# Stacking the recurrence gates of a hybrid attention and RG-LRU step on one Trainium2 core

## The reference

```python
z = rmsnorm(x, norm_mix_g) @ w_in             # 1024 -> c_q 768, c_kv 256, k_r 32, x_r 512, g_r 512
q = rmsnorm(c_q, q_norm_g) @ w_uq;  ckv = rmsnorm(c_kv, kv_norm_g);  kpe = rope(k_r)
xc = conv_b + causal_conv4(x_r)               # width 4, each channel by itself
r = sigmoid(blockdiag(xc, w_gate_a) + b_a)    # 8 diagonal blocks of 64 x 64
i = sigmoid(blockdiag(xc, w_gate_x) + b_x)
log_a = -8 * r * softplus(-lambda);  a = exp(log_a)
h_t = a_t * h_{t-1} + sqrt(1 - a_t^2) * i_t * xc_t
y = h * gelu(g_r)
```

## Time and profile before

| | |
|---|---|
| median of 3 runs | 2471.58 us (2470.5 to 2473.3) |
| the profiled execution's own time | 2471.83 us |
| its span, first to last instruction | 2470.0 us |
| TensorE busy | 2453.4 us, 99% |
| VectorE busy | 1802.2 us, 73% |
| ScalarE busy | 1218.8 us, 49% |
| GpSimd busy | 515.6 us, 21% |
| mean granted TensorE clock | 0.998 |

### The profile page before, as it was taken

One profiled execution on the slowest core, in us unless ns is written; L12 is line 12 of the kernel. 1 busy time (PEld: TensorE's weight loads), 2 busy tenths in 40 slices (PEclk: granted clock), 3 DMA queues, 4 the chain that ended last, 5 costly groups with the idle time before them and its releaser, 6 DMA issues.

```text
span 2470.0 us, 43918 instructions
## 1 busy us (share of the span) xinstructions
PE 2453.4 (99%) x17416; PEld 2369.0 (96%) x17416; DVE 1802.2 (73%) x2782; ACT 1218.8 (49%) x2197; POOL 515.6 (21%) x478
## 2 busy tenths in 40 slices
PE   9999999999999999999999999999999999999997
PEld 9999977899999999999999999779999999999997
DVE  8678767579776777677676797674887766776676
ACT  5455355535554454455524643554355544554455
POOL 0024255200112211220201232541001112211222
PEclk9999999999999999999999999999999999999999
DMA  4122201223347634663721222013135456545655
GB/s 162 53 60 73 61 11 38 82 61 109 88 92 140 122 86 99 134 120 89 226 90 53 68 64 61 11 38 95 55 115 109 88 117 131 112 88 113 131 115 171
DMA packets 104809, 230.39 MB, mean 93 GB/s; under 512 B 14832, under 2 KB 18256, under 8 KB 104608
## 3 DMA queue, kind: packets, MB, share of 16 engines
q0 software_dynamic: 43648, 89.14, 20.5%
q1 hardware_dynamic: 60816, 138.42, 17.7%
q10 hardware_dynamic: 144, 0.04, 0.0%
HBM read 144.03 MB, written 81.18 MB: 91 GB/s over the span
## 4 chain that ended last, share of the span: by engine, by line
PE 95%; DVE 2%; issue 1%; DMA 1%; ACT 0%; POOL 0%; SPq 0%; DVEq 0%; POOLq 0%
PE ps L968 28%; PE ps L1386 23%; PE ps L1337 23%; PE ps L1201 5%; PE ps L1216 5%; PE ps L1478 3%; PE ps L1271 2%; PE ps L1148 2%; PE ps L1449 1%; PE ps L1173 1%; PE ps L1080 1%; DVE xall L2828 0%; PE ps L997 0%; DVE msq L2196 0%; DVE mxp L2569 0%
## 5 line engine op out<-in xcount | busy, mean ns | idle before, releaser
L2859 DVE TENSOR_TENSOR wlo<-raw_all,whi 128x512 fp32r<-128x512 f32 (+1 forms) x420 | 270.5, 652 | 176.3 <-ACT whi L2007 173.8
L2007 ACT ACTIVATE whi<-raw_all 128x512 fp32r<-128x512 f32 (+1 forms) x420 | 248.6, 599 | 279.4 <-DVE raw_all L2992 88.0
L3359 POOL DMA_DIRECT2D x_scratch<-stage x224 | 199.7, 941 | 837.9 <-DVE stage L3002 693.4
L2060 ACT ACTIVATE stage<-ps 128x536 f32<-128x536 f32 (+1 forms) x224 | 135.4, 612 | 147.0 <-PE ps L1386 142.6
L3002 DVE TENSOR_TENSOR stage<-stage,ps 128x536 f32<-128x536 f32 (+1 forms) x168 | 118.9, 708 | 84.4 <-PE ps L1386 83.4
L1530 ACT ACTIVATE whi<-raw_all 128x1024 fp32r<-128x1024 f32 (+3 forms) x72 | 66.6, 926 | 230.4 <-PE ps L968 229.3
L2569 DVE TENSOR_REDUCE mxp<-ps 64x1 f32<-64x64 f32 (+11 forms) x384 | 140.4, 372 | 54.6 <-PE ps L1148 48.1
L968 PE MATMUL ps<-xgh,whi 128*128 128x358 f32 (+1 forms) x720 | 157.3, 327 | 0.0
L968 PE MATMUL ps<-xgl,whi 128*128 128x358 f32 (+1 forms) x720 | 156.6, 326 | 0.0
L968 PE MATMUL ps<-xgh,wlo 128*128 128x358 f32 (+1 forms) x720 | 156.6, 325 | 0.0
L968 PEld LDWEIGHTS ps<-xgl,whi 128*128 128x128 f32 x720 | 124.1, 189 | 0.0
(11 more groups left out here) (837 smaller groups left out, 7679.5 us busy)
## 6 DMA issues: line engine op xcount, KB each, us to landing
raw_all<-in_wst SPq DMA_DIRECT2D x233, 256.0 KB, 3.4
raw_all<-in_wst SPq DMA_DIRECT2D x78, 512.0 KB, 3.6
x_scratch<-stage POOLq DMA_DIRECT2D x112, 268.0 KB, 6.0
x_scratch<-stage POOLq DMA_DIRECT2D x112, 264.0 KB, 6.0
x_scratch<-xall POOLq DMA_DIRECT2D x24, 537.0 KB, 3.5
xall<-x_scratch SPq DMA_DIRECT2D x24, 537.0 KB, 9.2
xall<-in_xT SPq DMA_DIRECT2D x16, 537.0 KB, 6.8
raw_all<-in_wst POOLq DMA_DIRECT2D x30, 256.0 KB, 5.1
```

The lines of the kernel that those rows point to most:

```text
L2007: nc.scalar.activation(dst, src, ACT.Copy).then_inc(S["u_hi"], 1)
L2060: nc.scalar.activation(quarters(stage_of(L, g, i, n)[:, 0:N2]), src, ACT.Copy, scale=-1.0 if row else 1.0).then_inc(S["x_copy"], 1)
L2859: V.tensor_tensor(dst, src, hi.bitcast(F32), ALU.subtract).then_inc(S["u_lo"], 1)
L3359: pool.dma_start(x_scr[2 * i + row, :, a:b], stage_of(L, g, i, n)[:, 0:b - a], accum_op=ALU.add).then_inc(S[done], 16)
```

## The change

There are three parts.

Gates. Rows of the moving operand are stacked: `x_even` holds the high part of the even head in rows 0 to 63 and its low part in rows 64 to 127; `x_odd` holds the odd head the other way round. The weights of a head, its r and i matrices side by side, stand twice, one above the other. One pass then gives high weights by (high + low) input for both gates of one head, and a second pass gives the low weights. `gates(c)` is 2 x 2 passes. It now is one unit: the even head's result goes to banks 6 and 7 and the free end of the slot's third bank, the odd head's to the slot. The operations that split the input and read the gates work on 64 rows each, so there are more of them.

Order. Units and weight blocks now have the same numbers. `gate_r` and `gate_i` only read PSUM; the rest is `decay` and `normal`, later on ScalarE. On VectorE `split(15)`, the weights of the fourth gates, and the read of the rotary key stand ahead of `lru(2)`; the read of CQ0 stands behind it and behind `split(16)`. The rotation of the rotary key and the copies into `ckv` stand after `split(22)`; they stood before the first `cq_low`.

Roots. SUM_Y and SUM_Q use `log_rstd`, and VectorE's two reciprocals of 1074 columns per layer are gone.

The core of the diff, in which the numbers of units, the host's rearranged weights and the order on the other blocks are cut:

```diff
-U_XR, U_GR, U_GATE, U_CKV = [0, 1, 2, 3], [4, 5, 8, 9], [6, 10, 14, 18], [12, 13]
-U_KR, U_CQ = 16, [17, 20, 21, 22, 23, 24]
+U_XR, U_GR, U_GATE, U_CKV = [0, 1, 2, 3], [4, 5, 7, 8], [6, 9, 12, 15], [10, 11]
+U_KR, U_CQ = 13, [14, 16, 17, 18, 19, 20]
...
-    READ[U_GATE[_c]] = ("gate_r", _c + 1)
-    READ[U_GATE[_c] + 1] = ("gate_i", _c + 1)
+    READ[U_GATE[_c]] = ("gate_i", _c + 1)
...
                 def gates(c):
+                    u, b = U_GATE[c], B_GATE[c]
                     w("xc_lo", c + 1)
-                    for k in range(2):
-                        product(to_slot(U_GATE[c] + k), U_GATE[c] + k, B_GATE[c], 128 * k, [tok(xch)], [tok(xcl)])
+                    w("w_lo", b + 2)
+                    take(u)
+                    if c:
+                        w("gate_i", c)
+                    else:
+                        w("root", SUM_MIX)
+                    for i, part in enumerate((whi, wlo)):
+                        for dst, c0, c1 in even_gates(c, TOK):
+                            nc.tensor.matmul(dst, part[b % 2][:, 0:P], x_even[:, c0:c1], start=(i == 0), stop=(i == 1))
+                    for i, part in enumerate((whi, wlo)):
+                        for q in range(3):
+                            mm = nc.tensor.matmul(to_slot(u)(q), part[b % 2][:, P:2 * P], tok(x_odd)(q), start=(i == 0), stop=(i == 1))
+                    mm.then_inc(S["mm"], 1)
...
+                def gate(c, dst, e, bias):
+                    rest = even_gates(c, T)[1][0]
+                    nc.scalar.activation(dst[0:64, 0:SUM_END].rearrange("p (c n) -> p c n", c=2), ps[half(e), 6:8, :], ACT.Tanh, scale=0.5,
+                                         bias=bias[half(e), c:c + 1])
+                    nc.scalar.activation(dst[0:64, SUM_END:T], rest[half(e)], ACT.Tanh, scale=0.5, bias=bias[half(e), c:c + 1])
+                    return nc.scalar.activation(chunks(dst[64:128, :]), slot(U_GATE[c])[half(1 - e)], ACT.Tanh, scale=0.5, bias=bias[half(1 - e), c:c + 1])
```

ScalarE around the rotary key:

```diff
                 split(14)
                 gate_i(2)
                 xc_hi(3)
-                split(15)
                 w("mm", U_KR + 1)
                 nc.scalar.activation(chunks(kpe[0:64, :]), slot(U_KR)[64:128], ACT.Copy).then_inc(S["kr_lo"], 1)
+                split(15)
+                decay(2)
+                normal(2)
                 gelu_a(2)
                 gelu_b(2)
                 split(16)
                 gate_r(3)
+                gate_i(3)
                 split(17)
-                gate_i(3)
+                decay(3)
+                normal(3)
```

VectorE around the rotary key, and further down:

```diff
                 split(14)
                 xc_lo(3)
-                lru(2)
-                split(15)
                 w("mm", U_KR + 1)
                 w("kr_lo", 1)
                 V.tensor_tensor(chunks(kpe[0:64, :]), slot(U_KR)[0:64], chunks(kpe[0:64, :]), ALU.add).then_inc(S["kr_ev"], 1)
+                split(15)
+                lru(2)
+                split(16)
                 scaled(U_CQ[0], cq[0], rs, "cq_ev", LIVE)
-                split(16)
                 gelu(2)
                 split(17)
...
                 split(22)
+                w("table_in", 32)
+                w("kr_ev", 1)
+                link(V.tensor_tensor(kpe[0:64, 0:T], kpe[0:64, 0:T], rs[0:64, :], ALU.mult))
+                rotate(kpe[0:64, 0:T], t1[0:64, :], cosT[0:64, :], sinT[0:64, :], None)
+                link(V.tensor_copy(kpe[64:96, 0:T], kpe[0:32, 0:T]))
+                split(23)
+                sum_lo(xch, sqa, xcl, SUM_Q)
...
-                rstd(t3, SUM_Y)
-                split(24)
-                rstd(rs, SUM_Q)
+                w("rstd", SUM_Q)
```

ScalarE's roots:

```diff
                 split(23)
                 w("cq_sum", 5)
                 nc.scalar.activation(live(xcl), live(sqa), ACT.Copy).then_inc(S["sum_hi"], 1)
-                root(SUM_Y, t3, LRU)
+                w("sum", SUM_Y)
                 queries_out(0)
+                log_rstd(SUM_Y, t3, LRU)
                 split(24)
```

More of the change, by code:

```diff
@@ L189 @@
 DONE_AT = [CLOSE_DOWN.index((_m, 0)) + 1 for _m in range(8)]
-U_XR, U_GR, U_GATE, U_CKV = [0, 1, 2, 3], [4, 5, 8, 9], [6, 10, 14, 18], [12, 13]
-U_KR, U_CQ = 16, [17, 20, 21, 22, 23, 24]
-U_UQ, U_K, U_V = [25, 26, 27, 28, 29, 30], 31, 35
-U_OY, U_OO, U_MLP = [45 + _c for _c in range(8)], 53, 61
+U_XR, U_GR, U_GATE, U_CKV = [0, 1, 2, 3], [4, 5, 7, 8], [6, 9, 12, 15], [10, 11]
+U_KR, U_CQ = 13, [14, 16, 17, 18, 19, 20]
+U_UQ, U_K, U_V = [21, 22, 23, 24, 25, 26], 27, 31
+U_OY, U_OO, U_MLP = [41 + _c for _c in range(8)], 49, 57
 NU = U_MLP
@@ L628, in half, with even_gates @@
             return slice(64 * e, 64 * e + 64)
+        def even_gates(c, end):
+            rest = ps[:, 3 * slot_of(U_GATE[c]) + 2, CH:CH + end - SUM_END]
+            return (ps[:, 6, :], 0, 512), (rest, SUM_END, end), (ps[:, 7, :], 512, SUM_END)
         def first_tmp(m):
@@ L1557, in gate_r, with gate_i, decay @@
                         w("conv", 4)
-                    nc.scalar.activation(chunks(t1), slot(U_GATE[c]), ACT.Tanh, scale=0.5, bias=half_ba[:, c:c + 1]).then_inc(S["gate_r"], 1)
+                    gate(c, t1, 0, half_ba).then_inc(S["gate_r"], 1)
+                def gate_i(c):
+                    gate(c, t4, 1, half_bx).then_inc(S["gate_i"], 1)
+                def decay(c):
                     w("gate_r", c + 1)
@@ L1618, in _ @@
                 gate_r(0)
-                split(8)
                 gate_i(0)
                 xc_hi(1)
+                split(8)
+                decay(0)
+                normal(0)
                 split(9)
@@ L1626, in _ @@
                 gate_r(1)
-                split(11)
                 gate_i(1)
                 xc_hi(2)
+                split(11)
+                decay(1)
+                normal(1)
                 split(12)
@@ L1714, in _ @@
                 nc.scalar.activation(live(xcl), live(sqa), ACT.Copy).then_inc(S["sum_hi"], 1)
-                root(SUM_Y, t3, LRU)
+                w("sum", SUM_Y)
                 queries_out(0)
+                log_rstd(SUM_Y, t3, LRU)
                 split(24)
+                w("sum", SUM_Q)
+                queries_out(1)
+                w("ckv_full", 1)
+                for c in range(2):
+                    nc.scalar.activation(ckvh[c][:, :], ckv[c][:, :], ACT.Copy).then_inc(S["ckv_hi"], 1)
                 w("cq_ev", 6)
-                root(SUM_Q, rs, QL)
-                queries_out(1)
+                log_rstd(SUM_Q, rs, QL)
                 split(25)
@@ L2443, in _ @@
                 split(20)
[L2445 to L2460, removed]
                 def cq_low(c):
@@ L2477, in _ @@
                 split(22)
+                w("table_in", 32)
[5 more added lines that the diff above has]
+                sum_lo(xch, sqa, xcl, SUM_Q)
+                w("ckv_n", 2)
+                for c in range(2):
+                    V.tensor_copy(ckv[c][:, PAST_A:META2], past[:, c, :])
+                    V.tensor_copy(ckv[c][:, META2:OWN2], ckv[c][:, 0:NMETA])
+                    V.tensor_copy(ckv[c][:, OWN2:PAST_B], ckv[c][:, STREAM:TOK])
+                    V.tensor_copy(ckv[c][:, PAST_B:KEY_END], past[:, c, 0:NMETA])
+                    ins = V.memset(ckv[c][:, KEY_END:KW], 0.0)
+                ins.then_inc(S["ckv_full"], 1)
+                V.memset(kpe[:, KEY_END:KW], 0.0)
+                V.tensor_copy(kpe[0:96, META2:OWN2], kpe[0:96, 0:NMETA])
+                V.tensor_copy(kpe[0:96, OWN2:PAST_B], kpe[0:96, STREAM:TOK]).then_inc(S["kpe_copy"], 1)
                 w("kpe_copy", 1)
@@ L2481, in _ @@
                 V.memset(kpe[96:97, :], 1.0).then_inc(S["kpe_ones"], 1)
+                split(24)
                 w("kv_out", 32)
@@ L3244, in _ @@
                 cq_add(3)
+                cq_add(4)
+                cq_add(5)
                 w("kpe_copy", 1)
@@ L3438 @@
             put(B_GR[c], block(w_in[:, s3 + P * c:s3 + P * c + P]))
-            gate = np.zeros((P, 2 * P), f32)
-            for n, name in enumerate(("w_gate_a", "w_gate_x")):
-                for i in range(2):
-                    gate[64 * i:64 * i + 64, P * n + 64 * i:P * n + 64 * i + 64] = a[name][l, 2 * c + i]
-            put(B_GATE[c], gate)
+            even = [a[name][l, 2 * c] for name in ("w_gate_a", "w_gate_x")]
+            odd = [a[name][l, 2 * c + 1] for name in ("w_gate_x", "w_gate_a")]
+            put(B_GATE[c], np.tile(np.concatenate(even + odd, 1), (2, 1)))
         for c in range(2):
```

36 lines of the change are left out of this document (16 added, 20 removed).

## The result

The changed kernel takes 2478.47 us (median of 10 runs, 2476.58 to 2480.05) against 2471.77 for the kernel before: a ratio of 1.0027, 95% interval 1.0019 to 1.0035. It is slower, by its median more than the 0.2% that I had set as the limit, and above my range. Its profiled execution took 2479.4 us, with a span of 2477.6.

The account below looks back on a forecast made before the run. TensorE, busy 99% of the span, was taken as the bound. Each layer gains 3.4 us and gives back 3.2; two layers of 0.2 less some 0.1 make 0.3, so 2471.58 becomes 2471.3 us, range 2464 to 2477.

Parts of the forecast that it names:

- Gates, the direct gain: Gates 0 to 2: four passes for six put a layer 3.4 us ahead by the rotary-key product's end.
- The fourth gates: Before CQ1: TensorE waits 4.5 us for VectorE's read of CQ0, chain 18.3 us, 3.2 us given back per layer.
- rival B: Clock falls to 1.2 GHz in the wait before CQ1, costing 2.3 us per layer: 2475.9 us; chance 0.18.
- my own case: Whole kernel: gates' gain nearly given back at CQ1, 2471.3 us, its own range 2467.6 to 2473.8; chance 0.56.
- my signs of being wrong: Gap before CQ1 under 2 us, clock under 1 after it, or TensorE waiting at SUM_Q.
- Rival A: At CQ1: VectorE reads CQ0 in time, no wait, 4.7 us gained per layer: 2462.2 us; chance 0.14.
- The moved rotation: Before SUM_Q: sum_lo ready at 238.5 for 238.67, no wait, at most 0.3 us per layer.
- the roots: Two VectorE reciprocals of 6.86 us per layer removed; TensorE didn't wait for them, so gain 0.

Follow-up runs that it names:

- e5_filled_half: Changed kernel with 16 matmuls of ones put between TensorE's waits for the fourth gates and these gates: 2473.93 us, ratio 1.0008.
- e1: Changed kernel with 34 matmuls of ones put between TensorE's waits for the fourth gates and these gates: 2480.87 us, ratio 1.0034.
- e6_split_ahead: Kernel of e4_sum_later with ScalarE's split of block 19 moved ahead of the Tanh of the fourth gelu: 2467.46 us, ratio 0.9979.
- e9: Changed kernel with 10 matmuls of ones, as e5_filled_half has 16, ahead of the fourth gates: 2476.65 us, ratio 1.0015.
- e10: Kernel of e6_split_ahead with VectorE's read of the sixth query product behind the lower parts of the third and fourth query tiles: 2469.76 us, ratio 0.9989.
- experiment 3: Changed kernel with VectorE's read of CQ0 and split of block 16 inside lru(2), ScalarE's split(16) ahead of gelu_b(2): 2478.41 us, ratio 1.0025.
- experiment 4: Kernel of experiment 3 with the keys' sum of squares behind CQ3 and VectorE's work reordered: 2468.35 us; with two further reorderings, 2467.46 and 2469.76 us.
- e4_sum_later: Kernel of experiment 3 with the keys' sum of squares behind CQ3 and VectorE's query reads and block 18 split reordered: 2468.35 us, ratio 0.9984.

## Why the prediction was wrong

**Gates, the direct gain.** Right in kind, too large: 1.3, 1.0 and 0.7 us by the table, 3.1 in a layer for 3.4 (2.7 in the second). A pass of the even head costs 0.62 us (131.20 to 132.43 for two), not 0.493: its matmuls are of 512, 512 and 48 columns, and I had taken the pass of three equal ones, which the odd head has (0.49).

**The fourth gates.** The mechanism, its place and its releaser were right. The chain was 19.0 us for 18.3. The missing 0.7 is ScalarE's: 0.4 because gate reads and copies on 64 rows weren't covered after all, 0.1 in the copy of the key (1.09 to the next start) and 0.2 from `decay(2)` to the start of `lru(2)`, 5.12 us for the 4.94 that I had read off. TensorE was due at 155.21, so the wait was 5.06 for 4.5.

**The rival B, where the prediction failed.** I gave 0.18 to a fall of the clock in the wait, for "two waits that just reach that length", with a wait of my own that was longer than the 4 us after which the end of the kernel showed the clock down. By my own two numbers it should have been the main case. This is the step that failed: the sum holds a wait of 4.5 us in each layer, and no term for the clock behind it. The runs showed 2.1 and 1.9 us for it by the distance behind CQ1, and 4.5 us in all by the filler. Without it the time is 2473.93 (e5_filled_half), next to the 2473.8 at which my own case ended. The clock under 1 behind the wait was also one of my signs of being wrong. The rule that I cited beside it, in the Trainium skill, TensorE: Matmul & The Clock Gate, The HAM clock gate, says that the clock goes down in idleness and needs sustained work to come back. The trace agrees: down after 2.6 us without a matmul, back 4.5 us into CQ1. The price of B, 2.3 us per layer, came out near, with some luck: it was read off the 24 warm-up matmuls, and what the runs show varies from 1.5 to 2.7 with the time worked at the lower level. Nor does the clock column of the profile say "lower level" there, it has 1.00 for 0 to 3 and 3 to 6; it is their pace, 0.19 us each, against 0.117 for the same kind in e5_filled_half (3.73 us for 32). B's time, 2475.9, misses the result by 2.6: 1.3 of it is the longer chain (0.7 and 0.6), 1.0 the smaller gain of the gates (0.3 and 0.7), and the rest is what the cheaper clock (4.0 for 4.6) and the wait in the MLP leave.

**What else is in the difference.** The MLP product in the table waits, and before it didn't. TensorE's row for it, and ScalarE's row for the weights that it waited for:

```profile
1218.59 0.52 PE L1496 MATMUL ps<-fh,whi 128*128 128x268 f32 x2 [1.19 <-DVE wlo L2748]
1215.32 0.63 ACT L1906 ACTIVATE whi<-draw 128x512 fp32r<-128x512 f32 x1 [3.89 <-DMA draw<-in_wst]
```

VectorE's split waits for ScalarE's, and this one for a transfer of weights, 3.89 us, where it waited 2.42 before. Waits of 0.4 to 0.65 us stand at the same product in e1, e5, e6, e9 and e10, and none in the other five runs. Why the transfer is late isn't shown, nor that the change makes it so.

**Rival A's ground.** I wrote that no row in the chain can shrink by 4.5 us. That is so, and experiment 3 shows what it means: wherever the read stands, the chain is waited for. But my reading stopped at the first consumer. The gain was still to be had by letting TensorE take other work first (experiment 4), since the matmuls behind the gates don't all hang on the recurrence. In e6_split_ahead CQ1 starts at 154.96, 4.5 us before its start in the earlier trace rows. Of what the two layers gain so, 4.5 us are left in the time (2471.95 to 2467.46); part of the rest goes to waits like the one at 219.27 and the one in the MLP (0.51).

**The moved rotation and the roots.** Right as far as they went. SUM_Q starts at 241.49, 2.82 later than the earlier trace rows, just as all its neighbours do; the wait for the stores is there and delays no matmul:

```profile
249.34 2.93 DVE L2316 TENSOR_TENSOR ckvl<-ckv,ckvh 128x1296 fp32r<-128x1296 f32 x2 [4.30 <-DMA out_ckv_out<-ckv]
```

But the roots' "gain is 0" holds only for the pair. I had costed them where they stood, and not as the cover for the work put ahead of them. With the stacked gates and without the roots, the moved rotation costs 25 us (2503.74 against 2479.18 with both put back).

## What to carry to other kernels

A wait on TensorE has two prices, its length and the half-rate matmuls behind it: here 5.1 and about 2 us. Whenever a forecast contains a wait, look in the trace for an idle stretch that brought the clock down, and book the second price unless the wait is clearly shorter. Work taken off a full engine turns into a gain only as far as the other engines' chains let it run ahead: follow the chain past the first wait, and change the full engine's order so that what depends on the chain comes last.

## What the runs showed of the hardware

- In the profiled executions the clock fell in or just behind every wait of 2.67 to 10.19 us in the front of a layer, and in none of 1.34 us or less. The cost behind it was 1.5 us after the waits of 2.7, and 1.5 to 2.7 us after those of 3.8 and 4.9. It was 0.45 of the time that TensorE worked at the lower level.
- Float32 matmuls of ones, 128 by 128, are carried out as two of 0.113 us each (32 for 16, 68 for 34), one start to the next.
- The same third operation of `lru(2)` takes 3.05 us beside GpSimd's cube, in the changed kernel, and 1.27 us in e4_sum_later, where it starts at 155.96, after the cube (151.04 to 154.03). The reads from PSUM that are shown take 1.27 or 1.28 us.
